# Latent attention of a prompt and sample step, rewritten: transposed result, two heads in column halves, work between the steps

## What is computed

```python
q = (rmsnorm(cq, q_norm) @ w_uq).reshape(b, t, MLA_HEADS, 64 + 32)      # nope | rope
k_nope = jnp.einsum('bsc,chd->bshd', ckv, w_uk)                          # from the latent, rank 128
v = jnp.einsum('bsc,chd->bshd', ckv, w_uv)
# per block of 128 queries, causal:
sc = jnp.einsum('bqhd,bkhd->bhqk', qn, k_nope) + jnp.einsum('bqhr,bkr->bhqk', qr, kr)
p = jax.nn.softmax(jnp.where(mask, sc * scale, -jnp.inf), axis=-1)
o = jnp.einsum('bhqk,bkhd->bqhd', p, v)
```

## Time and profile before

| | |
|---|---|
| median of 3 runs | 2779.91 us (2779.53 to 2780.59) |
| the profiled execution, its own time | 2784.94 us |
| its span | 2782.9 us |
| TensorE busy (matmuls) | 2609.5 us, 94% of the span |
| TensorE weight loads | 2480.3 us, 89% |
| VectorE (DVE) busy | 1090.4 us, 39% |
| ScalarE (ACT) busy | 540.8 us, 19% |
| GpSimd (POOL) busy | 923.5 us, 33% |
| DMA queues of hardware | 227 MB, 24% of 16 engines |

### The profile page before, as it was taken

The page is one execution under the profiler, slowest core; times in us unless marked ns, Lnnn a source line. Parts: engine busy times, 40 slices in busy tenths (PEclk is TensorE's granted clock), DMA queues, the critical chain, the costliest instruction groups (busy, mean ns, idle before and its releaser), DMA issues.

```text
span 2782.9 us, 41157 instructions
## 1 busy us (share of the span) xinstructions
PE 2609.5 (94%) x16250; PEld 2480.3 (89%) x16250; DVE 1090.4 (39%) x1881; ACT 540.8 (19%) x1240; POOL 923.5 (33%) x468
## 2 busy tenths in 40 slices
PE   4999999999989999998998988979899999999996
PEld 3999999999979988997777757879799999999996
DVE  7132222222283653003555624384622222222226
ACT  4100000000032421123333413211210000000002
POOL 5333333333344333330000301234243333333332
PEclk9999999999999999999999888789999999999998
DMA  4121222122222332311220115344112211111111
GB/s 154 67 88 67 88 68 94 67 88 70 92 113 84 128 138 78 116 73 58 66 62 14 54 68 185 131 159 144 61 63 69 105 46 46 46 46 46 46 46 61
DMA packets 85099, 229.38 MB, mean 82 GB/s; under 512 B 8681, under 2 KB 47122, under 8 KB 83826
## 3 DMA queue, kind: packets, MB, share of 16 engines
q1 hardware_dynamic: 79082, 208.38, 21.9%
q10 hardware_dynamic: 5864, 18.70, 1.7%
HBM read 196.65 MB, written 74.39 MB: 97 GB/s over the span
## 4 chain that ended last, share of the span: by engine, by line
PE 52%; DVE 6%; issue 3%; DMA 2%; ACT 1%; POOL 1%; SPq 0%; DVEq 0%; ACTq 0%; POOLq 0%
PE ps L732 12%; PE ps L733 12%; PE ps L734 12%; PE ps L995 2%; PE ps L971 2%; PE ps L1171 1%; PE ps L1075 1%; PE ps L845 1%; PE ps L847 1%; PE ps L846 1%; PE ps L984 1%; DMA sgt<-scratch_gates 1%; PE ps L1136 1%; PE ps L1154 1%; PE ps L1030 1%
## 5 line engine op out<-in xcount | busy, mean ns | idle before, releaser
L732 PE MATMUL ps<-u_hi,w_hi 128*128 128x352 f32 (+1 forms) x2880 | 932.1, 324 | 27.3 <-DVE u_lo L408 20.2
L733 PE MATMUL ps<-u_lo,w_hi 128*128 128x352 f32 (+1 forms) x2880 | 924.1, 321 | 0.0
L734 PE MATMUL ps<-u_hi,w_lo 128*128 128x352 f32 (+1 forms) x2880 | 922.1, 320 | 0.0
L642 POOL TENSOR_TENSOR w_hi<-raw,zero 128x1024 fp32r<-128x1024 f32 x184 | 351.2, 1908 | 1327.3 <-PE ps L732 1109.8
L732 PEld LDWEIGHTS ps<-u_hi,w_hi 128*128 128x128 f32 x2880 | 545.0, 189 | 38.7 <-DVE u_lo L408 19.6
L733 PEld LDWEIGHTS ps<-u_lo,w_hi 128*128 128x128 f32 x2880 | 545.6, 189 | 0.5 <-issue 0.2
L734 PEld LDWEIGHTS ps<-u_hi,w_lo 128*128 128x128 f32 x2880 | 544.7, 189 | 0.0
L645 POOL TENSOR_TENSOR w_lo<-raw,w_hi 128x1024 fp32r<-128x1024 f32 x184 | 449.6, 2443 | 14.4
L1644 DVE TENSOR_TENSOR h<-ps,silu 128x352 f32<-128x352 f32 x132 | 68.1, 516 | 751.3 <-PE ps L734 746.1
L1653 DVE SCALAR_TENSOR_TENSOR x<-ps,x 128x352 f32<-128x352 f32 (+1 forms) x528 | 270.6, 515 | 211.3 <-PE ps L734 210.9
L732 PE MATMUL ps<-h_hi,w_hi 128*128 128x352 f32 (+1 forms) x1056 | 343.2, 325 | 10.8 <-DVE x L1653 8.3
(11 more groups left out here) (274 smaller groups left out, 2848.4 us busy)
## 6 DMA issues: line engine op xcount, KB each, us to landing
raw<-in_wstream SPq DMA_DIRECT2D x186, 512.0 KB, 3.3
out_win_out<-in_cache_win SPq DMA_DIRECT2D x23, 1424.0 KB
latn<-in_cache_mla SPq DMA_DIRECT2D x128, 80.0 KB, 1.9
scratch_gates<-stage ACTq DMA_DIRECT2D x16, 516.0 KB, 2.7
out_win_out<-in_cache_win SPq DMA_DIRECT2D x7, 1168.0 KB
kv_d<-in_cache_win SPq DMA_DIRECT2D x24, 256.0 KB, 9.4
sgt<-scratch_gates SPq DMA_DIRECT2D x16, 352.0 KB, 3.7
scratch_x_mid<-x SPq DMA_DIRECT2D x1, 4128.0 KB, 12.2
```

The costliest lines, as they stand in the source:

```text
L642: nc.gpsimd.tensor_tensor(hi, raw[:, s % RAW], zero[:].to_broadcast([P, UW]), ALU.add).then_inc(w_hi_done, 1)
L732: a = mm(out, wh, xh, start=start, stop=False)
L733: mm(out, wh, xl, start=False, stop=False)
L734: return a, mm(out, wl, xh, start=False, stop=stop)
```

## The change

Only the latent attention of the prompt, its splits before and its loads are rewritten; decode, dilated attention and the rest keep their instructions (they read the page buffer with `latent_slot(b)` in place of `b`).

- The splits of `cq` and `ckv`, and the rotary key rows of the first pair, are done before the gates. SP issues the first `pw_raw` load as soon as the last values of the dilated heads are out (`v_ready` 9), and POOL splits it behind the last gate unit.
- Buffers of queries, keys, values, `probs` and `probsT` are doubled over pairs or steps.
- The steps of all four pairs are one sequence of 64, the two heads of a query tile next to each other. The first pair's ten projection tiles run ahead of it; the other pairs' projections are done one tile per step (`filler`), through bank 7.
- DVE divides the probabilities themselves (`scale`) before they are transposed, not the result after.
- `values` works on 256 queries (two tiles) at once with the values stationary (64 columns each) and the transposed probabilities moving (256 columns, 128 for the last key block). Head 0 writes PSUM partitions 0 to 63 and head 1 partitions 64 to 127 of one bank. The result is transposed already: the eight transposes and `o_pair` are gone. ACT writes `om_hi`, DVE `om_lo`, four times per pair. `values` pieces stand in `filler` too.
- SP's page loops issue two pages per turn. Pages of sequences 4 to 7 go where the latents and weights of the projections lie, so their 64 loads wait for the last projection (`pj_ready` 40, in step 41). The decode weights stay behind them in SP's queue.

The diff, cut to its core:

```diff
@@ SP
-            sp.wait_ge(proj_ready, 96)
-            sp.dma_start(pw_raw[:], io["pairw"][0]).then_inc(pw_landed, 16)
             sp.wait_ge(const_landed, 16 * N_CONST)
             sp.wait_ge(x_kept, 16)
             sp.wait_ge(rope_add, 4 * 12)
-            sp.wait_ge(split_done, U_MIX)
+            sp.wait_ge(v_ready, 9)
+            sp.dma_start(pw_raw[:], io["pairw"][0]).then_inc(pw_landed, 16)
+            sp.wait_ge(proj_ready, 96)
             for p in range(4):
-                with sp.Fori(0, 2 * NPG) as j:
...
                 if p < 3:
                     sp.wait_ge(pw_split, p + 1)
                     sp.dma_start(pw_raw[:], io["pairw"][p + 1]).then_inc(pw_landed, 16)
-            sp.wait_ge(om_done, 9)
+                if p == 2:
+                    sp.wait_ge(pj_ready, 40)
+                with sp.Fori(0, NPG) as j:
+                    for k in range(2):
+                        page = sp.value_load(pages[0:1, bass.ds(2 * j + (2 * NPG * p + k), 1)], min_val=0,
+                                             max_val=io["cache_mla"].shape[1] - 1)
+                        sp.dma_start(latn[:, bass.ds(2 * j + (NPG * latent_slot(2 * p) + k), 1), :],
+                                     io["cache_mla"][0, bass.ds(page, 1)].rearrange("a p c -> p a c")
+                                     ).then_inc(latn_landed[p], 16)
+            sp.wait_ge(om_done, OM_MLA)
             sp.dma_start(wukT[:], io["wukT"]).then_inc(dec_landed, 16)
             sp.dma_start(wuv[:], io["wuv"]).then_inc(dec_landed, 16)
@@ planning
+        STEPS = [(h, n) for n in range(8) for h in range(2)]
+        def filler(S):
+            i, s = divmod(S, 16)
+            j = None
+            first = 4 if i == 0 else 0
+            if i < 3 and first <= s < first + 10:
+                j = 10 * (i + 1) + s - first
+            pv = {5: (4 * i, (0, 1)), 9: (4 * i + 1, (0, 1)), 10: (4 * i + 1, (2, 3)), 13: (4 * i + 2, (0, 1)),
+                  14: (4 * i + 2, (2, 3)), 15: (4 * i + 2, (4, 5))}
+            if i > 0:
+                pv.update({1: (4 * i - 1, (0, 1, 2)), 2: (4 * i - 1, (3, 4, 5)), 3: (4 * i - 1, (6, 7))})
+            k, kbs = pv.get(s, (None, ()))
+            return j, k, kbs
@@ TensorE
+            def values(k, kbs):
...
+                for kb in kbs:
+                    c0 = P if kb == 2 * g + 1 else 0
+                    for h in range(2):
+                        last = mm(ps[h * HD:(h + 1) * HD, 6, (k % 2) * 256 + c0:(k % 2) * 256 + 256],
+                                  v_pair[i % 2][:, kb, h * HD:(h + 1) * HD], probsT[k % 2][:, h, kb, c0:256],
+                                  start=kb == 0, stop=kb == 2 * g + 1, skip_group_check=True)
...
+            scores(0)
+            for S in range(N_MLA):
+                if S < N_MLA - 1:
+                    scores(S + 1)
+                j, k, kbs = filler(S)
+                if j is not None:
+                    pe.wait_ge(pj_act, pj_act_count(j - 1))
+                    pe.wait_ge(pj_dve, pj_dve_count(j - 1))
+                    projection(j, 7)
+                if k is not None:
+                    values(k, kbs)
+                transposes(S)
+            values(15, range(8))
@@ ScalarE
+            exponential(0)
+            for S in range(N_MLA):
+                if S > 0:
+                    copy_odd(S - 1)
+                if S < N_MLA - 1:
+                    exponential(S + 1)
+                j, _, _ = filler(S)
+                if j is not None:
+                    projected(j)
+                if pv_ends(S) is not None:
+                    keep_om(pv_ends(S))
+                if S < 4:
+                    rope_rows(1, S // 2, 64 + 32 * (S % 2))
@@ VectorE
+            def scale(S):
+                h, n = STEPS[S % 16]
+                w = (n + 1) * P
+                dve.wait_ge(probs_done, S + 1)
+                V.reciprocal(st_rden[:, S % 8:S % 8 + 1], st_den[:, S % 8:S % 8 + 1]).then_inc(rden_done, 1)
+                dve.wait_ge(rden_done, S + 1)
+                V.tensor_scalar(probs[S % 2][:, 0:w], probs[S % 2][:, 0:w], st_rden[:, S % 8:S % 8 + 1], None, ALU.mult
+                                ).then_inc(p_scaled, 1)
...
+            for S in range(N_MLA):
+                if S > 0:
+                    copy_even(S - 1)
+                scale(S)
+                if S < N_MLA - 1:
+                    row_max(S + 1)
+                j, _, _ = filler(S)
+                if j is not None:
+                    projected(j)
+                if pv_ends(S) is not None:
+                    om_lower(pv_ends(S))
```

More of the change, by code:

```diff
@@ new lines, in scores @@
+            def scores(S):
+                i, s = divmod(S, 16)
+                h, n = STEPS[s]
+                if S >= 2:
+                    pe.wait_ge(probs_done, S - 1)
+                if s == 0:
+                    pe.wait_ge(pj_act, pj_act_count(10 * i + 7))
+                    pe.wait_ge(pj_dve, pj_dve_count(10 * i + 7))
+                    pe.wait_ge(kT_rope, 4 if i == 0 else 10)
+                for a in range(0, n + 1, 4):
+                    w = min(4, n + 1 - a) * P
+                    bank = 2 * (S % 2) + a // 4
+                    diag = n < a + 4
+                    last = mm(ps[:, bank, 0:w], qT[i % 2][h][:, n * P:(n + 1) * P], kT[i % 2][h][:, a * P:a * P + w],
+                              start=True, stop=not diag)
+                    if diag:
+                        last = mm(ps[:, bank, w - P:w], identb[:], masks[:, P:2 * P], start=False, stop=True)
+                last.then_inc(scores_ready, 1)
@@ new lines, in _ @@
+            for j in range(10):
+                if 2 <= j < 8:
+                    pe.wait_ge(act_read, A0 + 42 + (j - 2) + 1)
+                if j == 8:
+                    pe.wait_ge(pj_act, pj_act_count(1))
+                    pe.wait_ge(pj_dve, pj_dve_count(1))
+                projection(j, 6 + j if j < 2 else j - 2)
+            scores(0)
[10 more added lines that the diff above has]
+                transposes(S)
@@ L1074, in _ @@
                 for j in range(NPG):
-                    last = mm(out, dprobsT[:, j, heads], latn[:, b * NPG + j, 0:P], start=False, stop=j == NPG - 1)
+                    last = mm(out, dprobsT[:, j, heads], latn[:, latent_slot(b) * NPG + j, 0:P], start=False, stop=j == NPG - 1)
                 last.then_inc(latn_read, 1)
@@ L1817, in _ @@
+            copy_even(N_MLA - 1)
+            om_lower(15)
             dv = Tally(dm_v)
```

430 lines of the change are left out of this document (205 added, 225 removed).

## The result

The changed kernel takes 2747.03 us (median of 4 runs, 2744.02 to 2750.08) against 2780.25 us for the kernel before in the same comparison: a ratio of 0.988, 95% interval 0.986 to 0.990. That is 33 us less, where 12.6 were forecast. The profiled execution took 2744.02 us, its span is 2742.2 us.

What follows compares the result with a forecast made beforehand. PE bound the old kernel (94% busy), DVE and ACT in series the new. Last projection 1435.5, 64 pages at 1.40 to 1526, decode matmul 1530.2, 12.6 us gained: 2779.91 - 12.6 = 2767.3 us, range 2749 to 2789.

Steps and rivals of the forecast that it cites:

- SP's queue decides the end: After the last projection, 64 pages, then decode weights load on SP: pages end at 1526; attention alone would allow 1517.
- the line: Start of the first matmul behind the decode weights, taken as finish: forecast at 1530.2 instead of 1542.8 us.
- the price of a page: SP's page loops, two pages per turn: 1.40 us per page, ends 1.36 and 1.67.
- the entry: Before the attention steps: early loads and splits remove 9 us of PE waiting and the slow matmuls; steps start at 1290.0.
- the ring: DVE and ACT in series each attention step (maximum, exp, `scale`): 1.48 us at 128 columns, 3.64 at 1,024.
- the time of the last projection: In the third pair of the prompt attention: 1290.0 + 52.9 + 54.9 + 29.7 = 1427.5 us, 1435.5 with 8 us added.
- To this I add 8 us for what such sums miss: Allowance on the last projection's time: 3 us per pair kept of 11 unexplained before, 8 us in all.
- the larger of two sums: Each attention step takes the larger of DVE/ACT's and PE's time: middle pair 54.9 us, first 52.9, last 44.3.
- Rival 1: Chance 0.20: pages at 1.36 us, column halves fully overlapping, no allowance; decode matmul at 1517, gain 26, time 2754 us.
- Rival 2: Chance 0.15: column halves in the value product run one after another, 15.3 us per pair; gain 2.7, time 2777 us.
- Rival 3: Chance 0.18: low PE clock in the attention steps, at mean 0.7 PE needs 62.7 us per pair; time 2787 us.
- Rival 4: Chance 0.07: overlap real but pages not last, SP issuing in under 1.25 us; the attention's end counts, 2754 us.

Runs made afterwards that it cites:

- Experiment 1: Changed kernel with the two decode weights loaded from ACT's queue instead of SP's: 2731.06 us.
- experiment 2: Changed kernel with SP's page loops issuing one page per turn instead of two: 2754.31 us.
- experiment 6: Changed kernel without the multiplication of the probabilities by the reciprocal of their sum: 2734.92 us.
- experiment 7: Kernel of Experiment 1 with DVE's low result part put off one step and its small `qs_all` copy one projection tile: 2725.88 us.
- experiment 3: Changed kernel, value products one head after the other per piece: 2747.15 us; both heads written into the same 64 PSUM partitions: 2755.07 us.
- experiment 8: Changed kernel with all ten projection tiles of the next pair together in step 14 instead of one per step: 2831.41 us.
- experiment 4: Changed kernel with DVE's row maximum of the next step ahead of this step's `scale`: 2774.11 us.
- experiment 9: Kernel of experiment 7 with DVE's small copy and addition of rotary query rows ahead of the two zero fills: 2722.39 us.

## Why the prediction was right and wrong

**Right: what sets the end.** "SP's queue decides the end" held: the pages begin behind the last projection, the weights behind the pages, and PE stood idle for 13.95 us at that matmul where "some 13 us" were forecast. Experiment 1 took the queue away and the line moved to where the attention's end puts it; experiment 2 moved it by the price of a page alone.

**Right: the entry.** The first projection came at 1277.56 (1278.1 forecast) at full clock. `scale(0)` ended at 1291.30 where the ring was to start at 1290.0: ACT loads an activation table for 1.28 us before the first exp, and the first `scale` took 0.97 us beside POOL's split.

**Right: the ring.** Maximum, exp and `scale` run in series, at the prices that were set (maximum 1.22, exp 1.11, `scale` 0.75 at 1,024 columns where 0.72 was estimated). Experiments 6 and 7 shorten it and the pairs get shorter. But it is a narrow bound: PE is idle for only some 4.5 of 52 us per pair, and in experiment 6 it takes over.

**Wrong: the time of the last projection.** This is the step that failed. It was forecast at 1427.5 + 8, with the first page at 1436.5; the first page came at 1420.58, 15.9 us earlier. Three terms of the sum make it up:
- "To this I add 8 us for what such sums miss": nothing was missed. The allowance was carried over from the 11 us per pair that PE's sum had not explained in the kernel before. There PE was idle for 6.6 of 62.5 us in the first pair and at half clock for some 26 us of the whole stage, behind the wait at the entry and the gaps between pairs; in the kernel after it is at half clock for some 6.8 us, and the waits for the ring were in the forecast's sum already. How the 11 us split I haven't measured. 8 us.
- The steps took 128.3 us up to the last projection instead of 137.5. A step of the ring takes 3.54 for 3.64 us at 1,024 columns and 1.4 for 1.48 at 128. With the measured `scale` its fixed part is 0.46 instead of 0.59; the parts that the forecast names add up to 0.56, not 0.59, and the rest is shorter hand-overs. At 0.1 us per step that is at most 4.1 us over 41 steps, an estimate that takes every step to be the ring's. The rest, some 5.1 us, lies in steps where the forecast took the larger of two sums, among them 0.134 for a value pass that costs 0.11. I haven't split it further.
- The entry, 1.3 us the other way.

**Wrong by a little: the price of a page.** 1.40 was chosen between 1.36 and 1.67, and it was 1.35, just under the lower end: 3.7 us less from the first page to the decode weights. With 0.2 us between the weights and the matmul that makes 15.9 + 3.7 + 0.2 = 19.8, and 1530.2 - 19.8 = 1510.4 is the line. So these sizes add up to the whole error of the line. The time itself came out 20.6 us below the forecast (33.2 for 12.6), which is the same within the scatter behind the line.

**The rivals.** Rival 1 (pages at 1.36, full overlap, no allowance) is what happened: all three of its conditions came true, and even its 1517 was 6.6 us late, since its 134.6 us of steps came to 128.3. Rival 2 (column halves one after another) is refuted by experiment 3; its price was about right, 8 us more of time and a first page 10.0 us later counted from the last gate matmul, where 9.9 were worked out. The rule of the Trainium skill behind it, that a weight load overlaps matmuls only where the row group differs (TensorE: Matmul & The Clock Gate, Part 3), is not what these rows show, and the measurement decides: two column halves of the same rows, each pass with its own weights, cost 0.11 us per pass against 0.216 for a pass on one half. The same part's table of measured packings, which the prediction left aside, has a speedup for column tiles too, 2.38 times for three, and with that these rows agree. Rival 3 (low clock in the steps) didn't occur in the changed kernel, whose clock was 1.00 in three of the four stretches. But its mechanism is real and near: in experiment 8 the clock of a PE with a wait at every tile fell to 0.57, and in experiment 4, with PE waiting in nearly every step, to 0.92 from 1291 to 1486 us. Rival 4 (pages not last) is false for this kernel, where a page takes 1.35 us. What it describes, an end set by the attention, appears in experiment 1, where the weights are moved, and in experiment 4, where the attention is slower.

The range missed by 2 us: its lower end lay 5 us below rival 1's price, which left too little for the steps' own unknowns, all of which were counted upward. By the forecast's own signs, the page at 1.35 instead of 1.4 us and the first page at 1420.6 instead of near 1435 told of the miss; the releaser (`wuv`) and PE's wait of over 10 us were as named.

## What to carry to other kernels

Before adding work behind a queue of register-driven loads, ask what stands at the queue's end: here two loads of decode weights behind 64 pages cost 11 to 12 us of waiting, and moving them to an idle engine's queue gave that back. Work with a hand-over per tile belongs between other work: ten tiles cost 7.7 us between the steps and 29 us in a row, where every tile waits and the clock stays at its lower level besides. And before reordering two operations on one engine, follow the ring through every engine's order, PE's included, as experiment 4 shows.

## What the runs showed of the hardware that was not expected

- Two column halves of TensorE in fp32 overlap completely: 0.11 us per pass of 256 columns against 0.216 on one half, and still so in groups of four passes per half. In groups of 6 and of 16, only four passes on each side of the change overlap, and the others run alone.
- DVE operations that read and write SBUF are held up beside a POOL operation, small ones too: 32x64 in 1.97 instead of 0.19 us, a zero fill of 128x1088 in 3.83 instead of 1.28, `scale` in 0.97 instead of 0.29 and once in 1.62 instead of 0.75. Operations of a single column were not (negation 0.15 and reciprocal 0.15 to 0.17 beside POOL as elsewhere), nor were those that read PSUM: row maxima of 1,024 columns 1.21 to 1.22, `om_lo` 0.42, copies of 512 columns 0.68 to 0.69. The Trainium skill states it as an exclusive lock on a port pair (SBUF — State Buffer, SBUF: two separate sides); the rows agree for the operations that were held up, and experiment 9 shows that the order on DVE decides who pays.
- PE's clock, once it had fallen behind a wait of 2.6 us, stayed at its lower level through a group of tiles in which PE was idle for only 0.7 of each 2.8 us, while the steps of the kernel after, with about 4.5 us of idle PE in 52, kept the full clock from 1299 us on.
